# Three edits around the jobs of up to 96 tokens in a one-core decoder layer: turns interleaved with products, bias loads merged, one bias load earlier

## What is computed

```python
def moe_ffn(h, w_router, b_router, w1, b1, w2, b2):      # 1024 tokens, top 4 of 32 experts
    logits = h @ w_router + b_router
    top_vals, top_idx = lax.top_k(logits, TOP_K)
    gates = jax.nn.softmax(top_vals, axis=-1)
    ...
    def expert_block(args):
        toks, gts, e = args
        hid = h[toks] @ w1[e] + b1[e]                    # (tokens, 1024) @ (1024, 2048)
        yb = clamped_swiglu(hid) @ w2[e] + b2[e]         # (tokens, 1024) @ (1024, 1024)
        return yb * gts[:, None]
    ...                                                  # the rows are added to their tokens

def clamped_swiglu(hid):
    x_glu, x_lin = hid[..., ::2], hid[..., 1::2]
    x_glu = jnp.minimum(x_glu, 7.0)
    x_lin = jnp.clip(x_lin, -7.0, 7.0)
    return x_glu * jax.nn.sigmoid(1.702 * x_glu) * (x_lin + 1.0)
```

## Time and profile before

| | us |
|---|---|
| median of 3 runs (1968.91 to 1974.28) | 1971.47 |
| the profiled execution | 1971.53 |
| its span, first to last instruction | 1969.7 |
| mixer, routing and wide jobs | 0 to 1272 |
| six slim jobs | 1272 to 1489 |
| eleven narrow jobs | 1489 to 1970 |

### The profile page before, as it was taken

The page is one execution under the profiler, slowest core; times in us unless marked ns, Lnnn a source line. Parts: engine busy times, 40 slices in busy tenths (PEclk is TensorE's granted clock), DMA queues, the critical chain, the costliest instruction groups (busy, mean ns, idle before and its releaser), DMA issues.

```text
span 1969.7 us, 33296 instructions
## 1 busy us (share of the span) xinstructions
PE 1910.2 (97%) x12224; PEld 1398.8 (71%) x12224; DVE 1303.0 (66%) x3759; ACT 411.8 (21%) x910; POOL 235.6 (12%) x317
## 2 busy tenths in 40 slices
PE   7999999997999999999999999999998999999996
PEld 5677777774999999999999999834333444444442
DVE  2787778774377777775666666645355767777665
ACT  1233332222121122222222222223221100001100
POOL 1212222221010111111111111110100000000000
PEclk8999999998999999999999999999999999999998
DMA  9411100113966778788888989999999999999992
GB/s 311 113 43 43 43 18 35 32 33 144 339 207 228 246 261 269 245 282 278 289 285 283 307 300 304 316 368 381 360 368 382 382 375 356 369 369 367 360 360 72
DMA packets 207682, 498.39 MB, mean 253 GB/s; under 512 B 7716, under 2 KB 14928, under 8 KB 200080
## 3 DMA queue, kind: packets, MB, share of 16 engines
q1 hardware_dynamic: 194016, 449.43, 63.7%
q0 software_dynamic: 11312, 39.85, 8.2%
q10 hardware_dynamic: 2304, 8.39, 1.0%
HBM read 470.24 MB, written 27.41 MB: 253 GB/s over the span
## 4 chain that ended last, share of the span: by engine, by line
issue 40%; PE 29%; DMA 5%; POOL 1%; DVE 1%; POOLq 0%; ACT 0%; DVEq 0%; ACTq 0%
PE ps_unit L1885 29%; DMA out_dram<-y_rows,idx_cur 4%; POOL x_got L1378 1%; DMA x_got<-h_rows,idx_next 0%; PE ps_list L1857 0%; POOL carrier L1374 0%; POOL out_dram L1435 0%; POOLq L1096 0%; POOLq L1290 0%; DVE match L1562 0%; DVE reached L1610 0%; POOL out_dram L1390 0%; POOLq L1426 0%; POOLq L1265 0%; DVE xT L1684 0%
## 5 line engine op out<-in xcount | busy, mean ns | idle before, releaser
L1885 PE MATMUL ps_unit<-xT,w_slot 128*128 128x136 f32 (+6 forms) x3840 | 521.5, 298 | 1.6 <-DVE xT L1684 1.6
L1885 PEld LDWEIGHTS ps_unit<-xT,w_slot 128*128 128x128 f32 x3840 | 516.6, 196 | 2.0 <-issue 2.0
L1915 PE MATMUL ps_unit<-w_slot,xT 128*128 128x512 f32 x704 | 306.7, 594 | 0.0
L1279 DVE STREAM_TRANSPOSE xT<-x_got 32x256 f32<-32x256 f32 x644 | 280.5, 436 | 12.1 <-DMA x_got<-h_rows,idx_next 3.7
L1885 PE MATMUL ps_unit<-act_T,w_slot 128*128 128x136 f32 (+6 forms) x1920 | 261.6, 298 | 0.1
L1885 PEld LDWEIGHTS ps_unit<-act_T,w_slot 128*128 128x128 f32 x1920 | 257.9, 190 | 2.2 <-DVE act_T L1659 1.5
L1915 PEld LDWEIGHTS ps_unit<-w_slot,xT 128*128 128x128 f32 x704 | 132.8, 190 | 163.0 <-issue 163.0
L1675 DVE STREAM_TRANSPOSE y_rows<-yT 32x256 f32<-32x256 f32 x372 | 162.1, 436 | 55.0 <-ACT yT L1481 50.1
L928 PE MATMUL ps_c<-hT,w_in_sb 128*128 128x128 f32 x1536 | 182.1, 279 | 4.3 <-DMA w_in_sb<-in_w_in_dram 4.3
L928 PEld LDWEIGHTS ps_c<-hT,w_in_sb 128*128 128x128 f32 x1536 | 177.3, 194 | 9.6 <-DMA w_in_sb<-in_w_in_dram 5.2
L1374 POOL TENSOR_TENSOR carrier<-carrier 128x1 f32<-128x1 f32 x64 | 14.5, 227 | 1319.1 <-issue 610.8
(11 more groups left out here) (294 smaller groups left out, 1790.5 us busy)
## 6 DMA issues: line engine op xcount, KB each, us to landing
w_slot<-in_w_dram SPq DMA_DIRECT2D x192, 2048.0 KB, 12.1
b_row<-in_b_dram SPq DMA_DIRECT2D x11, 1024.0 KB, 12.9
w_in_sb<-in_w_in_dram SPq DMA_DIRECT2D x6, 1024.0 KB, 12.0
b_row<-in_b_dram SPq DMA_DIRECT2D x11, 512.0 KB, 15.1
x_in<-in_x_dram SPq DMA_DIRECT2D x8, 512.0 KB, 3.5
x_res<-in_x_dram SPq DMA_DIRECT2D x8, 512.0 KB, 4.7
out_dram<-x ACTq DMA_DIRECT2D x8, 512.0 KB, 5.1
h_rows<-h ACTq DMA_DIRECT2D x8, 512.0 KB, 3.1
```

The source lines that it names most:

```text
L1279: last = nc.vector.transpose(out[c * Q:(c + 1) * Q, :, tokens], rows.rearrange("p (k c j) -> p k c j", c=P // Q, j=Q)[:, :, c, :])
L1885: last = pe.matmul(ps_unit[p % RING][:, u, 0:n], w, moving[:, k, 0:n], start=(k == 0), stop=(k == KD - 1))
L1915: last = pe.matmul(ps_hid[c], xT[:, k, 0:P], w_slot[:, c, k, :], start=(k == 0), stop=(k == KD - 1))
```

## The change

TensorE: round 0 is turned between round 2's k = 6 and k = 7 of layer one; layer two runs all of round 0 first, with the turn of round 1 between its halves and that of round 2 behind it, then rounds 1 and 2. A turn now also waits for the copy of the turn before. ScalarE copies round 2 before it waits for the b2 row. SP loads the four quarters of b1 for a slim job with one DMA whose source is (4, 32 repeats, 512) and whose destination is 128 partitions by 512. In the first narrow job alone, the wait for the last clip and the load of b1 stand behind the first weight load instead of the fourth.

```diff
-        b1_spread = event("b1_spread", 64)
+        b1_spread = event("b1_spread", 16)
...
-                    for g in range(W1_LOADS):
-                        src = b1[0, bass.ds(e, 1), g * LW:(g + 1) * LW].rearrange("o f -> (o f)")
-                        sp.dma_start(b1_row[g * TILE:(g + 1) * TILE, 0:LW], src.partition_broadcast(TILE)).then_inc(b1_spread.sem, 16)
+                    src = b1[0, bass.ds(e, 1), :].rearrange("o (g f) -> (o g) f", g=W1_LOADS)
+                    sp.dma_start(b1_row[:, 0:LW], src.unsqueeze(1).broadcast_to([W1_LOADS, TILE, LW])).then_inc(b1_spread.sem, 16)
...
-                with sp.Fori(0, narrow_jobs) as t:
+                def load_narrow(t, first_bias_behind):
...
-                        if i == W1_LOADS - 1:
+                        if i == first_bias_behind:
                             wait(sp, hid_read[W1_LOADS - 1], t + slim_jobs - 1)
                             src = b1[0, bass.ds(e, 1), :].rearrange("o f -> (o f)")
                             sp.dma_start(b1_row[:], src.partition_broadcast(P)).then_inc(b1_loaded.sem, 16)
...
+                load_narrow(0, 0)
+                with sp.If(narrow_jobs > 1):
+                    with sp.Fori(1, narrow_jobs) as t:
+                        load_narrow(t, W1_LOADS - 1)
...
                     slim_read_act(s, 1)
+                    slim_read_act(s, 2)
                     wait(act, b2_spread, s)
                     wait(act, cur_ready, q)
                     nc.scalar.activation(b2_row[0:SLIM, :], b2_row[0:SLIM, :], ACT.Copy,
                                          scale=gate_cur[0:SLIM, 0:1]).then_inc(slim_b2.sem, 1)
-                    slim_read_act(s, 2)
...
                 wait_round(pe, slim_rows, s, t)
+                if t > 0:
+                    wait_round(pe, slim_actT, s, t - 1)
...
                 for t in range(TILES):
-                    for k in (KD - 2, KD - 1):
-                        last = slim_first(t, k)
+                    slim_first(t, KD - 2)
+                    if t == TILES - 1:
+                        slim_turn(s, 0)
+                    last = slim_first(t, KD - 1)
                     last.then_inc(round_done.sem if t < TILES - 1 else w_used[W1_LOADS - 1].sem, 1)
-                for t in range(TILES):
-                    slim_turn(s, t)
+                slim_second(s, q, 0, range(0, 4))
+                slim_turn(s, 1)
+                slim_second(s, q, 0, range(4, KD))
+                slim_turn(s, 2)
+                for t in (1, 2):
                     slim_second(s, q, t, range(0, 4))
-                for t in range(TILES):
+                for t in (1, 2):
                     slim_second(s, q, t, range(4, KD))
```

## The result

The changed kernel takes 1980.5 us (median of 6 runs, 1978.75 to 1981.11) against 1971.52 us beside it on the same chip: ratio 1.0051, 95% interval 1.0041 to 1.0061, 9 us slower. The prediction was 1971.8 us. That is inside its range (1955 to 1981), at its edge, but the forecast was no change and the result is slower; of the rivals, (b) comes nearest in time, four engines that disturb more than the sum had, priced at up to 1984 us. The profiled execution took 1980.69 us with a span of 1978.9, 9.2 us over the span of before.

A forecast was written before the change was run, and what follows sets the result against it. It took TensorE to bound the narrow jobs and a DMA queue falling behind to limit the slim stage. Terms -1.1 + 7.5 - 6.1 = +0.3 us on the 1971.47 us median gave 1971.8 us, range 1955 to 1981.

The forecast's parts named there:

- (b): Rival, merged b1 load: four engines crowd each other in neighbouring partitions; up to +12.3 us, 1984 us; chance 0.17.
- Narrow jobs stay bound by TensorE and pass the shift on: Narrow jobs after the first: no time of their own added, earlier shifts reach the kernel's end unchanged.
- credit of 3.5 us in D: Merged load in slim stage: 3.5 us taken off the +11 us delay, since most engines run ahead of the slowest.
- D: Slim stage: shift of the slowest landing from merging four bias loads onto four engines; +7.5 us, bounds -4 to +19.5.
- Slim stage as a whole: All six slim jobs: 1.1 us gained with landings as before, 7.5 lost to the merged load; +6.4 us.
- The exchanged wait: Sixth slim job, after turn 1: removed stalls replaced by waiting for layer two's second half, landing 1477.0; only 1.1 us gained.
- Turns 1 and 2: TensorE, slim jobs: each turn costs 0.3 us instead of 0.99, 1.4 us less per job, period 33.4 us if TensorE-bound.
- Turn 0: Round 0's turn before round 2's last product: gain 0; late rows would hold that product by at most 0.44 us.
- First narrow job: Earlier bias row removes its stall: 41.71 us instead of 47.85, -6.1 us; the three delayed weight loads hide.
- the forecast case: Merged load on four engines, D from 1.4 to 13: no measurable change; chance 0.48.
- (a): Rival, merged load: sixteen engines carry it, crowding gone, slim stage ends 11.6 us earlier; 1954 us; chance 0.29.
- (c): Rival, first narrow job: its stall stays because its first loads come later; +6.4 us, 1978 us; chance 0.06.

The follow-up runs named there:

- merged load alone: Kernel before with only the four b1 bias loads of a slim job merged into one DMA of four source rows; 1981.91 us, ratio 1.0057.
- change with four loads: The changed kernel with the four separate 64 KB b1 bias loads again instead of the merged one; 1966.43 us, ratio 0.9980.
- turns alone: Kernel before with only the new orders on TensorE and ScalarE, four b1 loads and the old narrow bias order; 1965.3 us, ratio 0.9979.
- two engines: The changed kernel with the merged load's source as 2 rows repeated 64 times, only two bias quarters loaded; 1998.09 us, ratio 1.0139.
- the bias edit alone: Kernel before with only the first narrow bias load moved behind the first weight load; 1969.51 us, ratio 0.9990.

## Why the prediction was wrong, step by step

The forecast was +0.3 us and the medians differ by +9.0. Two steps failed. "Narrow jobs stay bound by TensorE and pass the shift on" put the second narrow job at nothing, and it costs +5.9 us. And the credit of 3.5 us in D, for the lead that most engines have, was not borne out (the merger alone delays the landings by 11.5 us, the sum without the credit gives 11); that the slim stage as a whole came out near the forecast is luck.

- *D, the merged load's delay.* Four engines was right, and their price of 2.2 us per job nearly so. The credit for the lead was not. Landings of each slim job's last weight load:

| slim job | 1 | 2 | 3 | 4 | 5 | 6 |
|---|---|---|---|---|---|---|
| before | 1280.6 | 1324.2 | 1362.6 | 1401.1 | 1439.2 | 1477.0 |
| merged load alone | 1279.4 | 1324.7 | 1365.7 | 1406.4 | 1446.8 | 1487.3 |
| change with four loads | 1280.6 | 1322.0 | 1360.1 | 1397.9 | 1435.1 | 1471.3 |
| the change | 1283.3 | 1326.2 | 1367.6 | 1407.1 | 1447.2 | 1487.1 |

The merger alone goes from 1.2 us ahead of before to 10.3 behind it: 11.5 us in five jobs, 2.3 a job, what the sum gives without the credit (11). Inside the change, against four loads, it goes from 2.7 to 15.8: 13.1 us. The change as a whole is 2.7 us behind before at the first job and 10.1 at the sixth, 7.4 more, which looks like D = +7.5 only because the turns moved the sixth job's landing forward by 5.7.

- *What a late landing costs.* The prediction priced one wait at one place and held the issue times fixed. TensorE pays waits of 1.63, 2.09, 1.82, 1.18 and 2.70 us in three jobs, three of them with slower blocks behind, and each wait makes later slots free later, so later loads are issued later (9.6 us for the last one). Meanwhile the sixteen engines together have less to do, which the sum had at nothing: from 1460 to 1500 us the DMA share is 1.04 before and 0.96 after, at 361 and 323 GB/s (windows of before, then of after):

```profile
1460.00:1500.00 40.00, 35.42 (x328) 15.76 (x319) 15.87 (x44) 9.04 (x20) 1.66 (x2) 0.96 1.04 361
```

```profile
1460.00:1500.00 40.00, 36.12 (x399) 14.09 (x392) 16.69 (x50) 10.16 (x24) 2.86 (x4) 0.96 0.96 323
```

- *Slim stage as a whole.* +6.4 forecast, +7.2 measured. So close only because two errors cancel. With four loads the stage takes 208.8 us, so the turns gave 7.7 us instead of the 1.1 allowed them, and the merger cost 223.7 - 208.8 = 14.9 instead of 7.5.
- *The exchanged wait* was treated as certain, with the landing held fixed at 1477.0. The profiles show that with the turns the landing can move forward too (1471.3 in the change with four loads, 1477.9 in turns alone, one execution each). "The wait is only exchanged" holds for the second of these and not for the first.
- *Turns 1 and 2.* Right: 0.37 us each against 0.3, no wait, period 33.57 against 33.4. *Turn 0* gained nothing by itself, as said; but "held by no more than 0.44 us" failed. In the fifth job TensorE idles 1.76 us before that turn, and 4.81, 5.29 and 3.29 us with two engines, while the version with four loads has no such idle time. VectorE's first add of that job starts 1435.94 - 1416.35 = 19.6 us after the job's start, against 1431.09 - 1413.22 = 17.9 before. I infer that it waited for the b1 row, since the idle time grows with fewer engines and is not there with four loads; the profile gives no landing of the merged load that would show it. A late row now holds layer one's last product with it.
- *Second slim job.* Not in the sum: it waits 4.19 us for its tokens and begins at the low clock (7.05 us for a block of 5.36), where before it waited 1.55. The wait is there in every version that has the turns (3.79 to 4.78 us) and not in the two that haven't (1.51 and 1.47); the first two jobs together take 73.14 us against 71.31. So there the turns cost 1.8 us where two periods should have saved 2.5. The gather of these tokens is issued 16.7 us after the first job's start in both kernels, but VectorE can begin with them 12.2 us behind that issue before and 13.6 after. Why they come later was not settled.
- *First narrow job.* Right to 0.1 us: 41.81 against 41.71, -6.0 against -6.1. Its three weight loads did hide behind the queue.
- *Second narrow job, the term put at nothing.* It is +5.9 us, and issuing its row sooner took 5.35 us off the change. "Narrow jobs stay bound by TensorE and pass the shift on" took the next job's margin as given. Before, the row of the second job landed at 1541.86, 1.8 us ahead of its first chunk (1536.59 + 7.05). With the bias edit alone it lands at 1544.00, 2.1 us later, while the job begins 6.1 us sooner: 6.5 us late. Taking a stall out of one job let the next one arrive before its own row, which is why the edit alone is worth 1.7 us.
- *Rivals.* (b) had the direction and comes nearest in time, but its mechanism is not what was seen. With its 0.155 us a packet and the full disturbance the merger would cost 3.9 us per job; it cost 2.3 alone and 2.6 inside the change, so it is the forecast case without the credit. The rest is the second narrow job, which no rival had. (a) was wrong for this source. For another source most of its gain is there: the load from 128 rows came to 1959.65 against its 1954. (c), the first job's stall staying, did not happen; it moved on by one job.

The sum of the measured terms: +2.1 + 7.2 - 6.0 + 5.9 = +9.2 us. Without the scatter ahead of the slim stage it is +7.1; the medians differ by 9.0, and where the other 1.9 us lie in them is open.

## What to carry to other kernels

Before you merge small broadcasts, look at the outermost count of the merged transfer. Here the same 256 KB per job as 4 rows lost 14 us against four separate loads, as 16 rows it was even with them, and as 128 rows it gained about 5, some 19 us less than as 4 rows. Where a queue is saturated, every later landing inherits the age of the slowest engine, so price a transfer by the engines that carry it and not by its bytes. And when a stall is taken out of one iteration, look up in the trace how much margin the next iteration's own load has; it had less than the stall, and most of the gain was handed on.

## What the runs showed of the hardware

- One broadcast of 256 KB per job, in 2 KB pieces, among weight loads: on two engines 1998.09 us, on four 1980.5, on sixteen 1965.9 as 16 rows and 1959.65 as 128 rows. Around the load the core gets 311 GB/s with 16 rows and 407 to 411 with 128.
- The number of engines that carry a load can be read from the page's count of packets under 512 B: 7716 with four loads, 7356 with one of four rows, 7344 with one of two, 7428 with one of 128.
- A broadcast row to 128 partitions disturbs the queue less than one to 96, though it has a third more bytes: 428 against 313 GB/s in the four us around its landing, and 431 against 282 in another pair of versions.
- Behind idle times of 1.82 to 4.37 us TensorE's next block of 1.93 us took up to 3.64 (the granted clock was 0.50, the 1.2 GHz level), but behind 1.18, 1.63, 1.98 and 2.17 us it took 1.93. The last idle time alone doesn't decide it: in the change with the second narrow bias sooner, a block behind only 1.10 us took 3.58, with an idle time of 2.07 shortly ahead. A stall costs its length and here up to 2.7 us more (8.02 us for a block of 5.36, behind 4.30 us).
